# A two-layer diffusion backbone: modulation tiles moved between stages, per-head factors kept rounded, a first stage in another order

## What is computed

```python
for l in range(DEPTH):                                   # DEPTH = 2, x_lat (1,512,1024), x_ctx (1,256,1024)
    mod_x = (silu(c) @ w_ada[l] + b_ada[l])[:, None, :]  # six vectors of 1024, and the same from c_ctx
    sh1x, sc1x, g1x, sh2x, sc2x, g2x = jnp.split(mod_x, 6, axis=-1)
    hx = modulate(rmsnorm(x_lat, g_attn[l]), sh1x, sc1x) # h * (1 + scale) + shift
    aqx, akx, avx, bqx, bkx, bvx = split_cols(hx @ w_in[l])
    # group A: 8 query heads on 2 key heads of 64; q, k normalised per head, rotated by position
    q = rmsnorm(aq.reshape(..., HEAD_DIM), g_q); k = rmsnorm(ak.reshape(..., HEAD_DIM), g_k)
    # group B: 4 heads, each the difference of two softmax maps, 128-wide values, rms-normed output
    x_lat = x_lat + g1x * (merge_heads(a_out_x, b_out_x, g_sub[l], lam_init) @ w_o[l])
    hx = modulate(rmsnorm(x_lat, g_ffn[l]), sh2x, sc2x)
    x_lat = x_lat + g2x * conv_ffn(hx, w_up[l], conv_w[l], conv_b[l], w_down[l])
    # the context tokens take the same way in layer 0; in layer 1 they only give keys and values
return rmsnorm(x_lat, g_final)
```

## Time and profile before

| | us |
|---|---|
| median of 3 runs | 1837.68 |
| lowest and highest | 1832.35, 1839.86 |
| the profiled execution | 1837.65 |
| its span in the trace | 1835.8 |
| TensorE busy in it | 1704.7 (93%) |
| VectorE busy | 1141.0 (62%) |
| ScalarE busy | 773.3 (42%) |
| GpSimd busy | 628.0 (34%) |

### The profile page before, as it was taken

The page is one execution under the profiler, slowest core; times in us unless marked ns, Lnnn a source line. Parts: engine busy times, 40 slices in busy tenths (PEclk is TensorE's granted clock), DMA queues, the critical chain, the costliest instruction groups (busy, mean ns, idle before and its releaser), DMA issues.

```text
span 1835.8 us, 26068 instructions
## 1 busy us (share of the span) xinstructions
PE 1704.7 (93%) x9596; PEld 1433.6 (78%) x9596; DVE 1141.0 (62%) x1742; ACT 773.3 (42%) x1269; POOL 628.0 (34%) x313
## 2 busy tenths in 40 slices
PE   4799998887979999999999999899888999999997
PEld 3667877666869888888888877688766888888887
DVE  6876777668687557576435674677754765154256
ACT  6525666444234331233123334566545353243243
POOL 0354662121013324232433315464122144444442
PEclk9898999899889999999999999899999999999999
DMA  8330000023313234344334432000012132322322
GB/s 343 109 103 24 24 24 24 12 84 141 131 66 117 81 103 138 115 126 136 127 115 126 137 126 93 24 24 24 24 35 86 53 104 92 99 95 94 101 91 92
DMA packets 45430, 168.22 MB, mean 92 GB/s; under 512 B 4740, under 2 KB 6788, under 8 KB 43544
## 3 DMA queue, kind: packets, MB, share of 16 engines
q1 hardware_dynamic: 40792, 156.46, 25.5%
q10 hardware_dynamic: 4544, 10.49, 1.6%
HBM read 161.69 MB, written 5.24 MB: 91 GB/s over the span
## 4 chain that ended last, share of the span: by engine, by line
PE 64%; DVE 6%; issue 3%; POOL 2%; ACT 1%; DMA 1%; DVEq 0%; ACTq 0%; SPq 0%; POOLq 0%
PE ps L1187 19%; PE ps L1188 19%; PE ps L1189 19%; PE ps L1305 2%; PE ps L1319 1%; POOL w_lo L1067 1%; DVE junk_mid L1987 1%; PE ps L1133 1%; DVE nb L2243 1%; PE ps L1338 1%; PE ps L1393 1%; DVE sqsum L2057 1%; PE ps L1339 1%; DMA w_raw<-w_d 0%; DVE pt_lo L2268 0%
## 5 line engine op out<-in xcount | busy, mean ns | idle before, releaser
L1067 POOL TENSOR_TENSOR w_lo<-w_raw,w_hi 128x1024 fp32r<-128x1024 f32 x177 | 450.7, 2549 | 985.3 <-ACT w_hi L1571 985.3
L1187 PE MATMUL ps<-h_hi,w_hi 128*128 128x512 f32 (+1 forms) x1592 | 568.2, 357 | 11.5 <-DVE h_lo L2092 10.2
L1188 PE MATMUL ps<-h_lo,w_hi 128*128 128x512 f32 (+1 forms) x1592 | 557.5, 350 | 0.0
L1189 PE MATMUL ps<-h_hi,w_lo 128*128 128x512 f32 (+1 forms) x1592 | 556.9, 350 | 0.0
L1187 PEld LDWEIGHTS ps<-h_hi,w_hi 128*128 128x128 f32 x1592 | 303.9, 191 | 62.6 <-issue 24.1
L1189 PEld LDWEIGHTS ps<-h_hi,w_lo 128*128 128x128 f32 x1592 | 303.5, 191 | 39.8
L1188 PEld LDWEIGHTS ps<-h_lo,w_hi 128*128 128x128 f32 x1592 | 304.3, 191 | 36.0
L1571 ACT ACTIVATE w_hi<-w_raw 128x1024 fp32r<-128x1024 f32 x188 | 198.3, 1056 | 250.2 <-PE ps L1189 226.3
L1187 PE MATMUL ps<-a_hi,w_hi 128*128 128x512 f32 (+1 forms) x552 | 191.6, 347 | 1.2 <-DVE a_lo L2452 1.2
L1188 PE MATMUL ps<-a_lo,w_hi 128*128 128x512 f32 (+1 forms) x552 | 191.3, 347 | 0.0
L1189 PE MATMUL ps<-a_hi,w_lo 128*128 128x512 f32 (+1 forms) x552 | 191.0, 346 | 0.0
(11 more groups left out here) (168 smaller groups left out, 2458.0 us busy)
## 6 DMA issues: line engine op xcount, KB each, us to landing
w_raw<-w_d SPq DMA_DIRECT2D x188, 512.0 KB, 3.5
ada_b<-ada_d SPq DMA_DIRECT2D x56, 512.0 KB, 4.3
...
x_sb<-x_d SPq DMA_DIRECT2D x1, 3072.0 KB, 12.4
x_sb<-x_d ACTq DMA_DIRECT2D x1, 3072.0 KB, 11.9
...
```

The source lines that it names most:

```text
L1067: nc.gpsimd.tensor_tensor(w_lo[:, c % RING, :], w_raw[:, c % RAW, :], w_hi[:, c % RING, :].bitcast(f32), ALU.subtract).then_inc(w_lo_done, 1)
L1187: nc.tensor.matmul(out, lh, rh, start=first, stop=False)
L1188: nc.tensor.matmul(out, lh, rl_, start=False, stop=False)
L1189: return nc.tensor.matmul(out, ll, rh, start=False, stop=last)
```

## The change

It has five parts.

1. **First stage.** x is loaded in two halves and squared as they land. Group 0 of the first modulation product is no longer split: TensorE multiplies it as eight plain fp32 products of 512 columns, ahead of the statistics. The pieces are twelve instead of sixteen, and the ring of `first_hi` has six places instead of three. The low parts of weight units 0 and 1 are made earlier on VectorE, those of units 2 and 3 move from GpSimd to VectorE, ahead of the bias and the gains. The last row copy comes after two `w_hi`.
2. **Head sums and factors.** The sums of a tile go in blocks of 256 tokens into three groups of 32 partitions, so the root and the reciprocal run on 96 x 256 instead of 10 x 768. Each sum stands there twice; ScalarE copies the factors as fp32r (RH, `head_hi`), VectorE makes from both a tile that holds the high part in one row and the low part in another (RL, `head_both`), and the spread is one fp32r product per block with 0/1 rows (`hot`), which VectorE copies once per layer. The load of `sel_rows` goes.
3. **Lead tiles.** `LEAD_MORE` = 6: tiles 24 to 29 are made beside the first projections too, after the eight of before. SyncE loads them between weight units 8, 9 and 10.
4. **Mid tiles.** Ten are left, none in the last head, and `MID_LATE` = [3, 3, 1, 1, 1, 1]; part 1 now stands between the factors and the loop of the group-B norm, parts 2 and 3 after the weight splits, one tile each after the first two updates. SyncE loads four of them ahead.
5. In the last head SyncE issues only weight loads.

```diff
-HEAD_ROWS = 2 * (B_TILE - 1)
+HEADS = B_TILE - 1
+QUAD, BLOCK = 32, 256
+N_BLOCKS = TOK // BLOCK
+HEAD_ROWS = QUAD * N_BLOCKS
-HI_RING = 3
+HI_RING = 6
-MID_ADA, MID_END = 3 * KT, 5 * KT
+LEAD_MORE = 6
+MID_ADA, MID_END = 3 * KT + LEAD_MORE, 5 * KT
-MID_EARLY = 5
-MID_LATE = [3, 2, 1, 1, 1, 1, 2]
+MID_LATE = [3, 3, 1, 1, 1, 1]
...
         plan["gate"] = op("DVE", "gate", .5, -20 + KT * .5, [ada[-1]])
+        for c in range(3 * KT, MID_ADA):
+            ada.append(op("DVE", "ada", 2.6, -3, [ada[-1]], c=c))
-    sd = op("ACT", "SD", 2.2, -6, [y["ST"] for y in normed])
-    rc = op("DVE", "SR", 1.2, -6, [sd])
-    plan["SD"], plan["SR"] = sd, rc
+    sd = op("ACT", "SD", 1.7, -6, [y["ST"] for y in normed])
+    rc = op("DVE", "SR", 1.7, -6, [sd])
+    rh = op("ACT", "RH", .4, -6, [rc])
+    both = op("DVE", "RL", .45, -6, [rh])
...
-            sp.dma_start(x_sb[:, :, :], x_in).then_inc(x_loaded, 16)
+            sp.dma_start(x_sb[:, 0:KT // 2, :], x_in[:, 0:KT // 2, :]).then_inc(x_half_loaded, 16)
+            sp.dma_start(x_sb[:, KT // 2:KT, :], x_in[:, KT // 2:KT, :]).then_inc(x_loaded, 16)
+            load_first(0)
+            load_first(1)
+            for n in range(RAW):
+                load_unit(n, first=True)
+            for g in range(2, n_first):
+                load_first(g)
...
-            pool.wait_ge(w_lo_done, RAW)
-            for n in range(RAW, RING):
-                split_unit(n)
+            pool.wait_ge(w_lo_done, RING)
...
+                    for b in range(y["width"] // BLOCK):
+                        mm = nc.tensor.matmul(ps[b * QUAD:(b + 1) * QUAD, 4, 0:BLOCK], sel,
+                                              a_sq[n % 2][:, b * BLOCK:(b + 1) * BLOCK], start=n == 0,
...
-                        mm = nc.tensor.matmul(ps[:, x["banks"][g], 0:t1 - t0], sel_rows[:, y["place"], :], head_r[:, t0:t1],
+                        mm = nc.tensor.matmul(ps[:, x["banks"][g], at:at + BLOCK], rows, head_both[:, :],
                                               start=True, stop=True)
...
+                for k in range(KT):
+                    if k % (KT // 2) == 0:
+                        pe.wait_ge(first_ada_loaded[2 * k // KT], 16)
+                    w = ada_first[:, 0:FIRST_GROUP, :].rearrange("p a k -> p (a k)")
+                    mm = nc.tensor.matmul(ps[:, 0, 0:width], silu_wide[:, k, :].bitcast(f32),
+                                          w[:, k * width:(k + 1) * width], start=k == 0, stop=k == KT - 1)
+                mm.then_inc(first_used, 1)
+                first_norm_stats()
+                for g in range(1, n_first):
...
             def first_norm():
-                first_pieces_lo(0)
+                for d in range(KT):
+                    add_squares(d, 0, TOK, d)
+                first_pieces_lo(1)
+                first_units_lo(0, RAW)
                 stats_scales(s, 0, n_tiles(norms[0]))
-                first_pieces_lo(1)
-                first_units_lo()
                 first_pieces_lo(2)
                 first_pieces_lo(3)
+                first_units_lo(RAW, RING)
...
                 stats_scales(s, 0, cols)
+                if l == 0:
+                    ada_late(1)
                 for b in range(B_HEADS):
...
-                    if l == 0:
-                        ada_late(3 + d)
+                    if l == 0 and 4 + d < len(MID_LATE):
+                        ada_late(4 + d)
```

168 lines of the change are left out of this document (86 added, 82 removed).

## The result

The changed kernel takes **1796.76 us** (median of 4 runs, 1795.55 to 1797.06), the kernel before beside it on the same chip 1837.65. The ratio is 0.9778, with a 95% interval of 0.9761 to 0.9795: 2.2% faster. The prediction was 1806, in a range of 1793 to 1829. The profiled executions took 1795.55 and 1837.65, with spans of 1793.7 and 1835.8, so the two traces have 42.1 us between them.

A forecast was written before the change was run, and what follows sets the result against it. TensorE works nearly all the time, so only places where it stands still or runs at half clock give time back. The terms -13 + 8 - 5 - 12 - 9.5 = -31.5 took 1837.65 to 1806 us, range 1793 to 1829.

The forecast's parts named there:

- first stage: Up to the first normalised tile: it starts at 44 instead of 57.27 us, -13, bounds -9 and -15.
- layer 0, until the first scores: Layer 0: twelve added streams delay the reciprocal, cheaper factors follow, and first scores come 5.9 us later.
- the colder clock: Layer 0: TensorE has stood about 15 us by the first scores, so 2 us are added.
- last head: Last head: ten streams go from VectorE and the waits for exponentials nearly whole, -5, bounds -2 and -7.
- output projection: Output projection: four of eight tiles go, the statistics wait falls and the clock rises, -12, bounds -7 and -14.
- layer 1: Layer 1: factors ready earlier, no wait for them, first scores at 1153 to 1155; -9.5, bounds -4 and -12.
- -4 for the halves of x: First stage: squares start on half of x, so the sums end at 19 instead of 23.06 us.
- Rival 1: First stage: TensorE becomes the bound through group 0's plain fp32 products, +9, 1815; chance 0.27 together with rival 2.
- Rival 3: Layer 0: the stand costs the first attention's clock and streams meet GpSimd, 52 us lost, 1850; chance 0.06.
- rival 4: Layer 0, milder form: streams of 2.4 us and a clock returning late, +14 and +8, 1820; chance 0.13.
- Rival 2: Output projection or layer 1: loads or ScalarE cover the removed work, +10, 1816; chance 0.27 together with rival 1.
- The quads: Layer 1's five sums of squares: about 0.5 us each side by side, 1.0 if not; -2.5 or 0.

The follow-up runs named there:

- x_whole: The changed kernel with ScalarE's squares waiting for the whole of x instead of its first half; 1797.69 us, ratio 0.9792 to the kernel before.
- late2: The changed kernel with the last two of its six added lead tiles placed behind the last factors' multiplication; 1800.54 us, ratio 0.9786 to the kernel before.
- No_tiles: The changed kernel with the new dealing of tiles undone, keeping the new first stage and head factors; ratio 0.9851 to the kernel before.
- early_cut: The kernel before with the ten streams of its last head cut to one column each, their loads kept; 1831.55 us, ratio 0.9970.
- order_kept: The changed kernel with the last head's ten old streams given back to the planner but not issued; 1801.43 us, ratio 0.9799 to the kernel before.

## Why the prediction came out right, point by point

The sum said -31.5 us and the traces show -42.1; the time fell inside the range, 9 us under the forecast. By its steps, where the +8 of layer 0 is taken apart into the 5.9 us by which the scores were to come later and the 2 us for a colder clock behind them:

| step | predicted | measured |
|---|---|---|
| first stage | -13 | -12.6 |
| layer 0, until the first scores | +5.9 | +3.3 |
| the colder clock (from there to the last head) | +2 | -0.4 |
| last head | -5 | -10.5 |
| output projection | -12 | -12.8 |
| layer 1 | -9.5 | -9.9 |
| the rest | 0 | +0.7 |

**The first stage** came out at its size, with one step of it wrong. The first tile is normalised from 44.71 on, the forecast said 44, and the gains, at 44.12, take 0.37 us instead of 3.88 with GpSimd idle. The bound that it named holds in its first half: ScalarE waits for the loads four times, 5.4 us in all, the last time ahead of 32.22, and from there until the bias ScalarE's and VectorE's own work sets the pace, with waits of half a us at most. But the -4 for the halves of x is worth nothing that x_whole can show. Rival 1, TensorE as the bound, did not happen: its sixteen records took 9.21 us, 0.58 each instead of the 1.03 that the rival counted, and it began at 17.34 when the first group had landed.

**Layer 0.** The mechanism is the predicted one: reciprocal later (80.35 behind the first projection against 65.65), TensorE standing 15.83 us before the spread, and a cheap way from there to the scores (9.29 us from reciprocal to scores, 20.71 before). The mis-sized term is the stream. It was taken at 1.97 us, the mean of sixteen; the twelve added ones took 20.3 us by their rows, 1.69 each, because five of the twelve took over 1.3 us and ten of those sixteen. With 1.69 and a read of 0.08, twelve make 21.2 us, less the 6.2 that were free: 15.0, measured 14.7, predicted 18.2. The way from the reciprocal to the scores was forecast at 8.4 and took 9.3.

The 2 us for a colder clock did not show. TensorE ran at the half level between the spread and the scores (granted clock 0.50 from 131.55 to 137.75), but so it did before (0.52). Behind the scores the clock came back as before, and from the first scores to the last head it took 263.05 us against 263.43 (262.65 to 264.99 in the other kernels, late2 apart, so a cost of one or two us could hide there). The 30 us from the first scores on, in before and then in after (columns as in the earlier trace rows):

```profile
147.02:177.02 30.00, 27.99 (x179) 22.48 (x179) 20.04 (x36) 17.67 (x35) 15.07 (x11) 0.91 0.05 18
```

```profile
137.75:167.75 30.00, 27.62 (x172) 22.08 (x172) 20.06 (x38) 18.48 (x36) 16.11 (x11) 0.89 0.06 20
```

No_tiles, which has no stand, has 0.91 too (123.30 to 153.30). The 0.96 of the earlier trace rows is for a stretch that begins 3 us behind the scores. Rival 3, which needed 39.5 us of loss here, is out with these rows, and so is rival 4, with its streams of 2.4 us and a clock that returns late. What a stand of more than 16 us would do, no run here shows.

**The last head** is where the sum was furthest off: -5 predicted with a lower end of -7, against -10.5. The step that failed is "they stand between the maxima, reciprocals and combinations": it counts the streams' time in one fixed order. early_cut and order_kept show that this time is about what was predicted (3.9) and that the rest came with the order that a planner without these streams chose (6.6), a term that the sum did not have. The order follows from the kernels alone, and it has the pairs of maxima torn apart in before and together in after; the prediction looked at VectorE's time only.

**The output projection** came out as forecast: the wait went from 10.66 to 1.24 us (predicted 1.5), and the 8 us behind it ran at a granted clock of 1.00 instead of 0.52. VectorE has 6.5 of 40 us free, and 2.99 of them it waits, by the profile, for the transfer of `c_bc`, a wait that the trace of before does not have. Rival 2 named such a cover; it is there, and it did not cost the gain.

**Layer 1**: no wait for the factors at 1113.76, scores 57.30 us behind the last statistics instead of 67.17. The new last wait is 3.11 us for the low half of a query. That one takes 0.68 us and stands behind the low half of the keys, which met a weight split of GpSimd:

```profile
1115.90 2.36 POOL L1075 TENSOR_TENSOR w_lo<-w_raw,w_hi 128x1024 fp32r<-128x1024 f32 x1
```

```profile
1116.40 2.67 DVE L2244 TENSOR_TENSOR ka_lo<-a_raw,ka_hi 128x768 fp32r<-128x768 f32 x1 [0.31 <-ACT ka_hi L1745]
```

**The quads.** The sums of squares of one tile, three blocks of 256 columns in three quads, in after; below it the same tile's 768 columns in before:

```profile
89.61 0.63 PE L1265 MATMUL ps<-a_sq,sm 128*32 128x256 f32 x6
```

```profile
94.73 1.46 PE L1259 MATMUL ps<-a_sq,sm 128*10 128x512 f32 x4
```

The quads run side by side, 2.3 times as fast, at a granted clock of 1.00 in both. Of the two rules of the Trainium skill that were set against each other, the one in TensorE: Matmul & The Clock Gate, Part 3 (2.38 times for three column tiles, there of 512 columns), agrees. Of the drain in TensorEngine Tiling (Array Packing), section Key Properties, nothing of a microsecond is to be seen: from the start of the last projection record ahead of the sums to the first one behind them it is 0.88 us, and 1.71 before.

**The range and the chances.** The forecast's own range, 1797 to 1816, ended 0.2 us above the result, and its five errors of 3, 5, 2, 3 and 3 us add as independent to 7.5 and not to the 9.5 that it has. The sizes that erred, by 2.6 us in layer 0, 2.4 for the clock and 5.5 in the last head, erred to the same side. The wider range reached down to 1793 for "the lower ends of the first term", and the first term came out as forecast; that the time lies in it for other reasons is luck. Two sums of the prediction do not come out of its own terms: the upper ends of all terms give 1830 and not 1836, and layer 0 with streams of 1.29 and 2.4 us gives 0 and +13 and not -1 and +14. None of this changes the forecast.
